# Time mixing's preparation inside the projections of a hybrid decoder block, and a fused add-and-minimum in sparse attention heads

## What is computed

```python
proj = xn @ w_comb                       # 1024 -> conv, attention, gate and time-mixing columns
# time mixing, on its 1792 columns p of proj
prev = jnp.pad(p, ((0, 0), (1, 0), (0, 0)))[:, :-1]
p = p + mu * (prev - p)                  # then split into r, k, v (512 each), xw, xa (64), xg (128)
log_decay = -DECAY_SCALE * jax.nn.sigmoid(w0 + jnp.tanh(xw) @ w_lora)
a = jax.nn.sigmoid(a0 + xa @ a_lora)
g = jax.nn.sigmoid(xg) @ g_lora
kk = heads(k * k_k)
kk = kk / jnp.maximum(jnp.linalg.norm(kk, axis=-1, keepdims=True), 1e-12)
k = k * (1.0 + (a - 1.0) * k_a)
...                                      # a scan over positions with r, exp(log_decay), k, v, kk, a
bonus = (jnp.sum(rh * kh * r_k, axis=-1, keepdims=True) * vh).reshape(b, s, w_)
return (out + bonus) * g, v_first

# sparse heads of the second block, each of three parts
s = jnp.einsum('bgrqd,bgkd->bgrqk', qi, kw) * SCALE + bias_win
p = masked_softmax(s, wmask)
```

## Time and profile before

| | us |
|---|---|
| median of 3 runs | 2189.09 |
| lowest and highest | 2185.13, 2189.16 |
| the profiled execution, its own time | 2187.5 |
| its span from first to last instruction | 2185.7 |

### The profile page before, as it was taken

The page is one execution under the profiler, slowest core; times in us unless marked ns, Lnnn a source line. Parts: engine busy times, 40 slices in busy tenths (PEclk is TensorE's granted clock), DMA queues, the critical chain, the costliest instruction groups (busy, mean ns, idle before and its releaser), DMA issues. The chain is left out here.

```text
span 2185.7 us, 29586 instructions
## 1 busy us (share of the span) xinstructions
PE 2055.5 (94%) x11804; PEld 1639.5 (75%) x11804; DVE 1122.3 (51%) x1747; ACT 786.3 (36%) x1277; POOL 125.6 (6%) x159
## 2 busy tenths in 40 slices
PE   8999667989999999999999989989999899999997
PEld 6888325877887977788888768886666678888886
DVE  5553765546445544567775344316766654423433
ACT  3111633243323433444443222134555544422421
POOL 0000404520000000000000000000000000000000
PEclk9999778999999999999999989979999999999998
DMA  4323000002332341223233432312111122223332
GB/s 174 96 96 99 22 1 2 3 2 95 97 97 88 116 138 39 78 96 96 96 96 109 161 100 92 97 49 69 33 36 40 58 88 90 97 98 98 98 98 77
DMA packets 49099, 175.56 MB, mean 80 GB/s; under 512 B 5248, under 2 KB 7680, under 8 KB 48736
## 3 DMA queue, kind: packets, MB, share of 16 engines
q1 hardware_dynamic: 46176, 164.05, 23.2%
q0 software_dynamic: 1664, 8.16, 1.1%
q10 hardware_dynamic: 1152, 1.89, 0.3%
HBM read 171.93 MB, written 2.15 MB: 80 GB/s over the span
## 5 line engine op out<-in xcount | busy, mean ns | idle before, releaser
L207 DVE TENSOR_TENSOR weights_lo<-weights_raw,weights_hi 128x1024 fp32r<-128x1024 f32 (+2 forms) x288 | 363.5, 1262 | 774.7 <-ACT weights_hi L199 774.3
L199 ACT ACTIVATE weights_hi<-weights_raw 128x1024 fp32r<-128x1024 f32 (+2 forms) x288 | 313.5, 1089 | 850.3 <-PE end_ps L232 245.6
L230 PE MATMUL sp_ps<-arena_parts,weights_hi 128*128 128x512 f32 x720 | 282.8, 393 | 3.0 <-DVE arena_parts L291 2.5
L232 PE MATMUL sp_ps<-arena_parts,weights_lo 128*128 128x512 f32 x720 | 281.0, 390 | 0.0
L231 PE MATMUL sp_ps<-arena_parts,weights_hi 128*128 128x512 f32 x720 | 280.9, 390 | 0.0
L230 PE MATMUL end_ps<-arena_parts,weights_hi 128*128 128x512 f32 x576 | 225.5, 392 | 2.2 <-DVE arena_parts L2880 1.7
L231 PE MATMUL end_ps<-arena_parts,weights_hi 128*128 128x512 f32 x576 | 224.9, 390 | 0.0
L232 PE MATMUL end_ps<-arena_parts,weights_lo 128*128 128x512 f32 x576 | 224.7, 390 | 0.0
L230 PE MATMUL fr_ps<-arena_parts,weights_hi 128*128 128x512 f32 (+1 forms) x480 | 182.8, 381 | 6.7 <-DVE arena_parts L291 2.4
L231 PE MATMUL fr_ps<-arena_parts,weights_hi 128*128 128x512 f32 (+1 forms) x480 | 181.0, 377 | 0.0
L232 PE MATMUL fr_ps<-arena_parts,weights_lo 128*128 128x512 f32 (+1 forms) x480 | 181.0, 377 | 0.0
(11 more groups left out here) (380 smaller groups left out, 3122.0 us busy)
## 6 DMA issues: line engine op xcount, KB each, us to landing
weights_raw<-w_up SPq DMA_DIRECT2D x44, 512.0 KB, 3.4
weights_raw<-w_proj SPq DMA_DIRECT2D x38, 512.0 KB, 3.5
weights_raw<-w_gates SPq DMA_DIRECT2D x32, 576.0 KB, 3.8
weights_raw<-w_ca SPq DMA_DIRECT2D x32, 512.0 KB, 3.4
weights_raw<-w_down SPq DMA_DIRECT2D x16, 704.0 KB, 4.0
weights_raw<-w_in SPq DMA_DIRECT2D x22, 512.0 KB, 3.4
weights_raw<-w_logits SPq DMA_DIRECT2D x16, 512.0 KB, 3.4
weights_raw<-w_ff1a SPq DMA_DIRECT2D x16, 512.0 KB, 3.4
```

Source lines behind the costliest of these rows:

```text
L199: act.activation(self.w_hi[:, g % 2, 0:cols], self.raw[:, g % 2, 0:cols], ACT.Copy).then_inc(self.hi_ready, 1)
L207: dve.tensor_tensor(self.w_lo[:, g % 2, 0:cols], self.raw[:, g % 2, 0:cols], self.w_hi[:, g % 2, 0:cols].bitcast(F32), ALU.subtract).then_ ...
L230: pe.matmul(out, left[0], right[0], start=start, stop=False)
L232: return pe.matmul(out, left[1], right[0], start=False, stop=stop)
```

## The change

1. `time_mix_stage` and `time_mix_scale_stage` are gone. Their work is in a new class `TimeMixIn`, whose methods are called from `proj_stage` after given groups (PE) or in given slots (ACT, DVE). PE's loop over groups is written out.
2. The groups of time mixing come in another order (`MIX_ORDER`): the narrow inputs, k, r, v. The blend with the previous position is now one ACT instruction (`share`) and one DVE instruction (`blend`) in place of three on DVE. Squares, and the factor of the key, move from DVE to ACT. The scans run in four pieces of 128 columns.
3. Low-rank rounds, norm, spread, bonus sums and transposes share the four banks of `proj_ps_v`, which before only the last four groups used; so each low-rank round waits until ACT has taken the one before (`lora_taken`).
4. Gate, bonus and the convolution's result go to device memory from GpSimd's queue (`Spill`), and are loaded back by SP: the convolution's result in `time_mix_chunks_stage`, bonus and gate at the start of `front_region`, ahead of `head_spread` and of the weights' stream. `exps` on ACT waits until the four gate tiles are stored, since it writes where they lay.
5. In sparse pairs the addition and the maximum become one `tensor_tensor_reduce` per head, which writes the negated sum and its running minimum; the exponential takes scale -1. Each is two instructions in the stream: the operation and a read of the accumulator. The forget pairs stay as they were.

```diff
+MIX_ORDER = [12, 13, 4, 5, 6, 7, 0, 1, 2, 3, 8, 9, 10, 11]
...
+class TimeMixIn:
...
+    def loras(self, pe, c):
+        cols = slice(c * P, (c + 1) * P)
+        if c == 0:
+            pe.wait_ge(self.wa_in, 16)
+            pe.wait_ge(self.g_in, 16)
+            pe.wait_ge(self.inner, 2)
+        else:
+            pe.wait_ge(self.lora_taken, c)
+        pe.matmul(self.ps[:, 0, :], self.lora[0:HD, cols], self.wa[0:HD, :], start=True, stop=True)
+        pe.matmul(self.ps[:, 1, :], self.lora[HD:P, cols], self.wa[HD:P, :], start=True, stop=True)
+        pe.matmul(self.ps[:, 2, :], self.g_lora[:, cols], self.xg, start=True, stop=True).then_inc(self.lora_out, 1)
...
+    def norm_spreads(self, pe):
+        pe.wait_ge(self.spread_in, 16)
+        pe.wait_ge(self.norm_ready, 1)
+        pe.wait_ge(self.lora_taken, NW)
...
+    def take_loras(self, act, c):
+        act.wait_ge(self.lora_out, c + 1)
+        act.activation(self.decay[:, c, :], self.ps[:, 0, :], ACT.Sigmoid, bias=self.core.v("w0", c))
+        act.activation(self.rate[:, c, :], self.ps[:, 1, :], ACT.Sigmoid, bias=self.core.v("a0", c))
+        act.activation(self.gate[:, c, :], self.ps[:, 2, :], ACT.Copy).then_inc(self.lora_taken, 1)
...
+    def exps(self, act, c):
+        act.wait_ge(self.gates.out, 16 * NW)
+        act.wait_ge(self.before_made, c + 1)
...
             @block.tensor
...
-                pe_gemm(core, pe, 31, KD, x, ps)
-                pe.wait_ge(scale.ready, 1)
+                for n in range(3, 34):
+                    pe_gemm(core, pe, 1, KD, x, ps)
+                    if n == 4:
+                        pe.wait_ge(scale.ready, 1)
+                        pe.wait_ge(const_in, 16)
+                    if 4 <= n < 8:
+                        tm.loras(pe, n - 4)
+                    if n == 8:
+                        tm.norm_sums(pe)
+                    if n == 10:
+                        tm.norm_spreads(pe)
+                    if n in (15, 16, 17, 19):
+                        tm.bonus_sums(pe, (15, 16, 17, 19).index(n))
+                    if 26 <= n < 32:
+                        tm.turn(pe, 2 * (n - 26))
+                        tm.turn(pe, 2 * (n - 26) + 1)
+                pe.wait_ge(tm.placed, 12)
                 pe_by_token(core, pe, 4, T, x, NT, lambda i, half: ps_v[:, i, :])
...
             @block.scalar
...
                 for n in range(2, 38):
                     core.split_hi(act, g0 + n + 2)
+                    if n == 2:
+                        share(0)
+                    if n <= 14:
+                        share(n - 1)
+                    if n == 3:
+                        tm.inner_gates(act)
+                    if 5 <= n < 9:
+                        tm.take_loras(act, n - 5)
+                    if 4 <= n < 8:
+                        tm.squares(act, n - 4)
+                    if n == 9:
+                        tm.root(act)
+                    if 10 <= n < 14:
+                        tm.exps(act, n - 10)
+                    if n in (13, 14, 15, 17):
+                        tm.factors(act, (13, 14, 15, 17).index(n))
+                    if 27 <= n < 33:
+                        tm.place(act, 2 * (n - 27))
+                        tm.place(act, 2 * (n - 27) + 1)
...
             @block.vector
...
+                def mixing(n):
+                    if n in (6, 8, 10, 12):
+                        tm.sum_up(dve, n // 2 - 3)
+                    if n == 8:
+                        tm.take_norm(dve)
+                    if n == 9:
+                        tm.invert(dve)
+                    if n == 11:
+                        for c in range(NW):
+                            tm.normalize(dve, c)
+                    if n in (14, 15, 16, 18):
+                        tm.keys(dve, (14, 15, 16, 18).index(n))
+                    if n == 14:
+                        tm.receptances(dve, 0)
+                        tm.receptances(dve, 1)
+                    if n in (15, 16):
+                        tm.receptances(dve, n - 13)
+                    if n in (16, 18, 21, 22):
+                        tm.bonuses_of(dve, (16, 18, 21, 22).index(n))
+                    if n in (19, 21, 22, 24):
+                        tm.scaled_keys(dve, (19, 21, 22, 24).index(n))
...
     def sync(self, sp):
+        self.core.spilled["spilled_bonus"].load(sp, self.bonus, self.bonus_back)
+        self.core.spilled["spilled_gate"].load(sp, self.gate, self.gate_back)
         sp.dma_start(self.spread, self.core.dram["head_spread"]).then_inc(self.spread_in, 16)
...
                     else:
-                        dve.tensor_tensor(s, bank(p)[:, :, 0:x.n], x.add, ALU.add).then_inc(biased, 1)
-                        dve.wait_ge(biased, p + 1)
-                    dve.tensor_reduce(stat(p, 0), s, AX.X, ALU.max, negate=True).then_inc(max_ready, 1)
+                        for side in range(2):
+                            ins = dve.tensor_tensor_reduce(s[:, side, :], bank(p)[:, side, 0:x.n], x.add[:, side, :], -1.0, 3.0e38,
+                                                           ALU.add, ALU.min, stat(p, 0, side, 1))
+                            ins.then_inc(biased if side else biased_first, 1)
```

More of the change, by code:

```diff
@@ L375, in proj_stage @@
     value = core.arena[:, 34:38, :]
-    conv = core.arena[:, 38:50, :]
-    diff = core.arena[:, 50:52, :]
+    plain = core.arena[:, 50:52, :]
+    rest_mu = core.small[:, 60:74]
     scale_at = core.arena[:, MIX_SCALE, :]
@@ L408, in _ @@
                 sp.dma_start(core.const[:, first_cols:], core.dram["const"][:, first_cols:]).then_inc(const_in, 16)
-                sp.dma_start(core.arena[:, 53, :], core.dram["wa_lora"]).then_inc(wa_in, 16)
-                sp.dma_start(core.arena[:, 54, :], core.dram["g_lora_t"]).then_inc(g_in, 16)
+                tm.sync(sp)
                 core.preloaded["proj"] = 2
                 core.stream(sp, "proj")
+            @block.gpsimd
+            def _(pool):
+                for c in range(NW):
+                    tm.gpsimd_gate(pool, c)
+                tm.gpsimd_bonus(pool, 0)
+                for c in range(NW):
+                    pool.wait_ge(conv_ready, c + 1)
+                    spilled_conv.store(pool, c, core.arena[:, c, :])
+                    if c < 3:
+                        tm.gpsimd_bonus(pool, c + 1)
+                pool.wait_ge(spilled_conv.out, 16 * NW)
+                pool.wait_ge(tm.bonuses.out, 16 * NW)
+                pool.wait_ge(tm.gates.out, 16 * NW)
             @block.tensor
@@ L532, in _ @@
                     if 1 <= n < 15:
-                        shift(n - 1)
+                        blend(n - 1)
+                    mixing(n)
                     if n >= 17 and (n - 17) % 3 == 0 and (n - 17) // 3 < NW:
@@ L954, in time_mix_chunks_stage, with _ @@
         with nc.Block() as block:
+            @block.sync
+            def _(sp):
+                core.spilled["spilled_conv"].load(sp, a[:, 0:NW, :], conv_back)
+                sp.wait_ge(conv_back, 16)
             @block.tensor
@@ L3055 @@
     stick_breaking_stage,
-    time_mix_stage,
-    time_mix_scale_stage,
     time_mix_chunks_stage,
```

422 lines of the change are left out of this document (212 added, 210 removed).

## The result

| | before | after |
|---|---|---|
| median of 4 executions each | 2187.64 us | 2169.18 us |
| lowest to highest | 2185.13 to 2189.16 | 2165.15 to 2169.47 |
| profiled execution, its span | 2185.7 | 2167.5 |

The ratio after to before is 0.9912, with a 95% interval of 0.9895 to 0.993: 18.5 us less, where the forecast was 2171.2. The ratio is clear of 1, and the difference between forecast and result (2 us) is less than the after kernel's own scatter (4.3 us). A fourth execution of the kernel before has joined the three that are shown ahead, which moves its median from 2189.09 to 2187.64.

The account below looks back on a forecast made before the run. TensorE was taken to bound the projections, the two removed stages being a chain through three engines. 65.0 - 25.1 - 10.8 - 0.1 - 1.9 - 10.8 = 16.3 off 2187.5 gave 2171.2 us; own range 2166 to 2176, eight in ten 2157 to 2179.

Parts of the forecast that it names:

- products added on TensorE: Projections: low-rank rounds, sums of squares, spread, bonus sums and transposes put between groups lengthen TensorE's path by 25.1 us.
- three waits for the taking: Projections, behind groups 5 to 7: TensorE waits 3.6 us for ScalarE's taking at each of rounds 1 to 3, 10.8 us.
- round 0's wait for the sigmoid: Projections: the first low-rank round waits for tanh and sigmoid with two table loads, 0 to 0.4 us, taken as 0.1.
- spread's wait for the reciprocal: Projections, behind group 10: the norm's spread waits for VectorE's reciprocal from slot 9, 1.9 us.
- clock behind the three waits: Projections: TensorE's clock falls behind each wait of 3.6 us and costs 2.5 us each time, 7.5 us.
- clock behind the spread: Projections: TensorE's clock falls behind the inverse norm's eight-row spread, costing 3.3 us.
- sparse heads: Pairs of heads: the fused operation lightens VectorE without changing the time, 0; bounds a gain of 9.8 and a loss of 2 us.
- spills, VectorE's and ScalarE's length: Stores and loads back land in time (0 to 2 us), and laced VectorE and ScalarE work hides behind TensorE's groups: 0.
- the lacing doesn't wait: Rival, projections: ScalarE's takes land ahead of the rounding and the change does what it was drawn to do, 2151; chance 0.04.
- A delay of GpSimd by VectorE: Rival, gate stores: VectorE's two-port operations hold up GpSimd's DMAs, and late stores hold ScalarE in slot 10; chance 0.02.
- may overrun by about 3 us once: Projections: a VectorE slot can run about 3 us long once, as a group's low part is due two groups later.
- the maximum is not in that chain: Sparse pairs: TensorE's 13 waits on the normalizing, 9.8 us, don't pass through the maximum, so 0 is gained.
- The slow fused operation: Rival, sparse pairs: at up to 6.5 ns a column the fused operation makes the kernel slower, 2190 to 2225; chance 0.04.

Follow-up runs that it names:

- experiment 1: Changed kernel with ScalarE taking each low-rank round's results ahead of that slot's rounding of weights: 2151.11 us, ratio 0.9837 to the kernel before.
- experiment 8: Changed kernel with the sparse heads as before, a separate addition and maximum in place of the fused operation: 2169.58 us, ratio 0.9922 to the kernel before.
- experiments 1 to 3: Changed kernel with ScalarE's taking ahead of rounding and share, ahead of the share only, or all but the gate ahead of rounding: 2151.11, 2165.81, 2157.02 us.
- experiment 4: Changed kernel with the inverse norm's spread behind group 11 in place of group 10: 2166.19 us, ratio 0.9898 to the kernel before.
- experiment 7: Changed kernel with ScalarE taking ahead of rounding and the spread cut in four pieces behind groups 11 to 14: 2148.77 us, ratio 0.9823.
- experiment 3: Changed kernel with decay and rate taken ahead of the rounding of weights and only the gate behind it: 2157.02 us, ratio 0.9857.
- experiments 9 and 10: Changed kernel with VectorE making the scaled copy one or three times more in each of slots 14 to 24: 2176.83 and 2178.15 us, one execution each.
- experiment 10: Changed kernel with VectorE making the scaled copy three times more in each of slots 14 to 24: 2178.15 us, one execution.
- experiments 3, 6 and 7: Changed kernel with only the gate taken behind rounding, or all taken ahead and the spread in four behind groups 10 to 13 or 11 to 14: 2157.02, 2153.63, 2148.77 us.

## Why the prediction was right

The forecast was 2171.2, the result 2169.18, in the forecast's own range of 2166 to 2176. Term by term:

| term | predicted | measured | from |
|---|---|---|---|
| products added on TensorE | 25.1 | 25.2 | 48.96 less the waits and the clock |
| three waits for the taking | 10.8 | 10.4 | waits of after; experiment 1 takes them away |
| round 0's wait for the sigmoid | 0.1 | 0.4 | waits of after |
| spread's wait for the reciprocal | 1.9 | 1.7 | waits of after |
| clock behind the three waits | 7.5 | 7.9 | 9.99, 9.87, 9.84 against 7.27 |
| clock behind the spread | 3.3 | 3.4 | stretch 109 to 117 |
| **sum on the projections** | **48.7** | **48.96** | |
| stages taken out | 65.0 | 64.96 | |
| sparse heads | 0 | -2.7 at equal clock | experiment 8 |
| stick-breaking stage | 0 | +1.8 | table of borders |
| spills, VectorE's and ScalarE's length | 0 | 0 | no wait, below |

The products' 25.2 is what remains when the other rows are taken off, and no measurement of its own. One low-rank round alone can be measured in experiment 1: two rounds that wait for nothing start 7.58 us apart, with one group of about 5.42 between them, which leaves 2.16 for the round, against 2.11 predicted.

**The waits** came out as derived from one slot and the pitch of ScalarE's instructions. The reason for them, the place of the taking behind rounding and share, is shown by experiments 1 to 3: each instruction moved ahead shortens the wait by its own pitch, 3.46, 2.85, 1.69, none. The prediction's rival "the lacing doesn't wait" is this case, and its 2151 is near experiment 1's 2151.11. But its sum leaves out the 1.9 of the spread's wait, which experiment 1 still has (1.75); with it the rival is 2153, so that the agreement to the microsecond is luck.

**The clock** had the right size, though its mechanism was half known. That the eight-row spread lowers the clock by itself, read from 492 to 504 us, is confirmed by experiment 4, and by experiment 7, where the same products spread over four groups keep it. That each wait of 3.6 costs about 2.5 was the middle of two neighbours and is a mean only: at 3.46 us it was 1.6 to 2.8 where the clock fell, and once 0. The Trainium skill (TensorE: Matmul & The Clock Gate, section "HAM oscillation — how this bites in real kernels") has such waits cost in every pass of a loop. The changed kernel's trace agrees in three of three rounds with 3.46 us; that of experiment 8 in two of three, and that of experiment 3, with 1.7 us of wait, in none.

**The spills** cost nothing, as predicted. The gate's four stores were issued at 53.1, 67.0, 80.7 and 94.4 us. The last column is the median time from issue to landing; the second of them took 4.2 us, the others 3.3. ScalarE's first exponential comes at 108.38 us directly behind its table load:

```profile
spilled_gate<-arena POOLq DMA_DIRECT2D x4, 256.0 KB, 3.3
```

```profile
107.08 1.28 ACT L507 ACT_TABLE_LOAD   x1
108.38 0.63 ACT L507 ACTIVATE arena<-arena 128x512 f32<-128x512 f32 x1
```

So the last store had landed some 9 us ahead of that load. The loads back cost nothing either: bonus and gate, issued at 460.80 and 461.18, took 4.8 and 7.0 us to land, and the bonus is first used at 470.63. A delay of GpSimd by VectorE, for which the prediction names the Trainium skill (SBUF — State Buffer, section "SBUF: two separate sides"), doesn't appear: each issue took 0.54 to 0.72 us. Whether any of VectorE's operations beside them ran in such a mode, no run here shows.

**VectorE's cover** was right for the changed kernel (no wait on it) and thinner than the sum said: "may overrun by about 3 us once" holds for the low part, but the bonus sums of experiments 9 and 10 want their operand before that.

**The sparse heads** are the term that was mis-sized. The step "the maximum is not in that chain" is wrong for a part of the waits: over the stage 19 of them became 15, and 13.1 us became 11.2; in the stretch of the earlier trace rows 13 waits and 9.8 us became 9 and 8.1, where the prediction wanted the 13 still there. It is right for the rest, since most waits on the normalizing stay with VectorE busy 25 us less. I had counted 10 to 20 us for that relief; it is 24.7. The fused operation ran near the addition's rate, and its second instruction, the read of the accumulator, costs no time of its own. In the changed kernel's trace, stretch 1529 to 1704:

```profile
L2921 DVE CUSTOM_DVE_ANT_0 arena<-pa_ps,arena 128x31 f32<-128x31 f32 (+4 forms) x96 | 33.6, 387 | 33.4 <-PE pa_ps L2818 33.4
L2921 DVE DVE_READ_ACCUMULATOR2_ANT arena<- 128x1 f32 x96 | 8.0, 83 | 0.0
```

33.6 us for the 21472 columns is 1.56 ns each with the 96 starts in it, against the addition's 1.39 with 48. The lengths of both groups add up to 41.6, but a read begins before the record of its operation ends: the table of stretches, asked for this line alone (window, length, VectorE's busy time, clock, DMA share, GB/s), has VectorE busy for 33.95 us:

```profile
1529.00:1704.00 175.00, 33.95 (x192) 1.00 0.11 37
```

So 34 us stand in place of 59.5. The slow fused operation, the rival that would have made the kernel slower, is far off.

**Not predicted at all:** the stick-breaking stage took 1.8 us longer on the same instructions, and between the profiles of this study it took from 57.3 (the kernel before) to 61.6 us. It begins with idle time and low clock, and where the low stretches fall in it varies. The 2 us between forecast and result are made of such differences, of the 2.7 of the sparse heads and of the 1.8 here; that they nearly cancel is luck.

## What to carry to other kernels

When work is laced between the groups of a busy TensorE, its products cost their length and that can be summed; what decides is what the helping engine does first. An instruction that frees TensorE's banks belongs ahead of any rounding for two groups later, and here that order was worth as much again as the whole change (18 us). A wait of 1.7 us in such a loop was paid once here, waits of 2.9 and 3.5 us mostly one and a half to two times; and products of a few rows are better spread over groups that don't wait than run in a row.

## What the runs showed of the hardware that I had not expected

- The clock's answer to equal waits is not the same each time: behind 3.46 us it fell in 14 of 15 cases looked at (changed kernel, experiments 4, 8, 9 and 10), and cost 1.6 us or 2.6 to 2.8, and once nothing. Nor do shorter waits fall in order: 1.69 kept it (three times), 1.88 kept it and 1.95 lowered it (both in experiment 10), 2.4 us of idle time in the kernel before kept it, and 2.85 lowered it (three times). Four executions of one kernel lay 2 to 10 us apart here; how much of that is the clock I can't say, since one of each was profiled.
- Eight-row products of 512 columns lower the clock with no idle time at all: it fell about 2.4 us into the spread of experiment 4 (0.83 in the mean from 110 to 112 us, 0.50 from 112 on), while TensorE was busy without a gap. The sums of squares, which use all 128 rows, kept it at 1.00 for 3.5 us in the same kernel.
- Two things that each keep the clock can lower it together: 1.7 us of wait, and 1.1 us of eight-row products (experiments 3, 6 and 7). The fall was seen once, in the one trace that has a single piece behind a wait.
- VectorE's addition with a running extremum does its columns at 1.56 ns, starts included. The read of its accumulator shows as an instruction of 83 ns, but it lies within the operation's own time: 192 instructions whose lengths add up to 41.6 us keep VectorE busy for 33.95.
